# One weight's low part moved from VectorE to GpSimd, and new instruction orders on ScalarE and VectorE

## What is computed

```
def even_mixer(h, w_in, w_out, ...):
    q, k, v, g_att, u_ssm, g_ssm = split(h @ w_in)        # w_in: 1024 x 5120
    q = apply_partial_rope(q) * HEAD_DIM ** -0.5           # the "rotary"
    k = apply_partial_rope(k)
    att = dilated_attention(q, k, v)
    ssm = s5_ssm(u_ssm, a_re, a_im, log_dt, b, c, d_skip, glu_w, glu_b)
    return concat([att * silu(g_att), ssm * silu(g_ssm)]) @ w_out
x = x + rmsnorm(even_mixer(rmsnorm(x)))      # layer 0 of block one
x = x + rmsnorm(odd_mixer(rmsnorm(x)))       # layer 1 of block one
for layer in range(2):                       # block two
    h = h + hybrid_mixer(rms_norm(h), ...)
    h = h + expert_choice_ffn(rms_norm(h), ...)
return rms_norm(h, final_norm_g)
```

## Time and profile before

| | |
|---|---|
| median of 3 runs | 1636.35 us (1635.52 to 1637.13) |
| the profiled execution | 1636.07 us, its span 1634.2 us |
| PE busy | 1307.5 us (80%) |
| DVE / ACT / POOL busy | 574.0 / 453.5 / 137.4 us (35% / 28% / 8%) |
| HBM read | 513.33 MB, 315 GB/s over the span |
| chain that ended last, by engine | DMA 45%, PE 38%, DVE 11%, ACT 2%, issue 2% |

### The profile page before, as it was taken

The page is one execution under the profiler, slowest core; times in us unless marked ns, Lnnn a source line. Parts: engine busy times, 40 slices in busy tenths (PEclk is TensorE's granted clock), DMA queues, the critical chain, the costliest instruction groups (busy, mean ns, idle before and its releaser), DMA issues.

```text
span 1634.2 us, 28359 instructions
## 1 busy us (share of the span) xinstructions
PE 1307.5 (80%) x12516; PEld 923.0 (56%) x12516; DVE 574.0 (35%) x873; ACT 453.5 (28%) x580; POOL 137.4 (8%) x169
## 2 busy tenths in 40 slices
PE   8999999999999987566666667999987556565665
PEld 6789889998989743223222234889843223232232
DVE  7993774765484520000000001584521001000001
ACT  5337654445554311001010012555311001010011
POOL 0220200000314000000000000304000000000000
PEclk9999999999999999988899897999999988899878
DMA  8334344545435899999999999335899999999997
GB/s 279 104 129 155 117 172 155 200 163 204 155 139 197 371 426 426 428 428 428 428 429 428 429 428 405 139 113 222 344 427 427 427 429 429 428 428 428 429 426 301
DMA packets 79503, 515.59 MB, mean 316 GB/s; under 512 B 6544, under 2 KB 6928, under 8 KB 54592
## 3 DMA queue, kind: packets, MB, share of 16 engines
q1 hardware_dynamic: 76000, 509.21, 76.4%
q0 software_dynamic: 912, 2.83, 0.5%
q10 hardware_dynamic: 2512, 2.36, 0.4%
HBM read 513.33 MB, written 1.05 MB: 315 GB/s over the span
## 4 chain that ended last, share of the span: by engine, by line
DMA 45%; PE 38%; DVE 11%; ACT 2%; issue 2%; SPq 1%; DVEq 0%; ACTq 0%
DMA board<-in_w_down 24%; DMA board<-in_w_gate 21%; PE dense L1750 8%; PE dense L1752 8%; PE dense L1751 8%; PE bank L2321 4%; PE bank L2351 2%; DVE ring_parts L1273 2%; DMA ring<-in_even_w_in 1%; DVE board L1556 1%; ACT ring_parts L883 1%; DVE board L1547 1%; PE dense L1773 1%; PE bank L2144 1%; PE bank L2291 1%
## 5 line engine op out<-in xcount | busy, mean ns | idle before, releaser
L2321 PE MATMUL bank<-ring,board 128*32 128x256 f32 x2688 | 207.4, 459 | 145.7 <-DMA ring<-in_w_up 82.5
L2321 PEld LDWEIGHTS bank<-ring,board 128*32 128x32 f32 x2688 | 90.4, 124 | 257.1 <-DMA ring<-in_w_up 104.2
L1107 ACT ACTIVATE board<-bank 128x256 f32<-128x256 f32 x32 | 12.3, 384 | 731.7 <-PE bank L2321 731.7
L1273 DVE TENSOR_TENSOR ring_parts<-ring,ring_parts 128x4096 fp32r<-128x4096 f32 (+1 forms) x43 | 181.6, 4228 | 88.6 <-ACT ring_parts L883 88.5
L1663 DVE TENSOR_TENSOR board<-board,bank 128x256 f32<-128x256 f32 x32 | 13.5, 421 | 553.3 <-ACT board L1107 553.3
L883 ACT ACTIVATE ring_parts<-ring 128x4096 fp32r<-128x4096 f32 (+1 forms) x47 | 161.5, 3438 | 123.7 <-DMA ring<-in_w_in 31.7
L1750 PE MATMUL dense<-board_parts,ring_parts 128*128 128x256 f32 x624 | 179.4, 288 | 0.5 <-DVE ring_parts L1273 0.5
L1752 PE MATMUL dense<-board_parts,ring_parts 128*128 128x256 f32 x624 | 176.6, 283 | 0.0
L2321 PE MATMUL bank<-board 128*32 128x256 f32 x1408 | 108.8, 461 | 65.4 <-DMA board<-in_w_up 40.7
L1750 PEld LDWEIGHTS dense<-board_parts,ring_parts 128*128 128x128 f32 x624 | 119.7, 192 | 1.9 <-issue 1.6
L1752 PEld LDWEIGHTS dense<-board_parts,ring_parts 128*128 128x128 f32 x624 | 119.6, 192 | 0.0
(11 more groups left out here) (354 smaller groups left out, 2057.3 us busy)
## 6 DMA issues: line engine op xcount, KB each, us to landing
ring<-in_w_gate SPq DMA_DIRECT2D x44, 2048.0 KB, 41.4
ring<-in_w_up SPq DMA_DIRECT2D x40, 2048.0 KB, 41.6
ring<-in_w_down SPq DMA_DIRECT2D x40, 2048.0 KB, 41.0
board<-in_w_up SPq DMA_DIRECT2D x24, 2048.0 KB, 41.0
board<-in_w_gate SPq DMA_DIRECT2D x20, 2048.0 KB, 40.5
board<-in_w_down SPq DMA_DIRECT2D x20, 2048.0 KB, 40.7
ring<-in_w_in SPq DMA_DIRECT2D x18, 2048.0 KB, 7.8
ring<-in_even_w_in SPq DMA_DIRECT2D x9, 2048.0 KB, 8.6
```

Source lines behind the costliest of these rows:

```text
L1273: tt(lo, slot_of(u), hi.bitcast(F32), ALU.subtract).then_inc(lo_done, 1)
L2321: last = mm(o.rearrange("p (m b) -> p m b", b=2), xeT[:, 4 * (j // 2) + k, :], cols.rearrange("p (m r b) -> p r m b", r=2, b=2)[:, q % 2], ...
```

## The change

- **Unit 4's low part**: DVE's `low_part(4)` between `whole_block(7)` and `states(0)` is gone. POOL makes it in one `tensor_tensor`, after `hi_done` has counted unit 4 and ahead of the rotary of q, with a signal of its own, for which PE waits before unit 4. The running count `lo_done` leaves unit 4 out.
- **ACT around units 1 and 2**: the copy `u_steps` moves ahead of `high_part(2)`; the three small transfers that ACT issues (masks and router weights) then come before `high_part(2)` too.
- **DVE around units 1 and 2**: the low part of unit 1 moves behind the products of the next round (`times`), and the low part of unit 2 likewise.
- **First seam**: DVE does `add_rows(1)` before tile 0's low part instead of behind it; unit 15's low quarters 0 and 1 move behind tile 1's gain.
- **Second seam**: of the next unit's low quarters, one instead of two stands between `add_rows(1)` and `normalise(1)`.
- **Experts' ends**: ACT's mean square goes by halves (`rms_halves`, L787), each half waiting for its own `x_ready`.

```diff
-            return sum(4 if v in QUARTERED else 1 for v in SPLIT if v <= u)
+            return sum(4 if v in QUARTERED else 1 for v in SPLIT if v <= u and v != POOL_LOW)
...
             gp.wait_ge(rest_in, 16)
+            gp.wait_ge(hi_done, SPLIT.index(POOL_LOW) + 1)
+            hi, lo = slot_of(POOL_LOW, True)
+            g.tensor_tensor(lo, slot_of(POOL_LOW), hi.bitcast(F32), ALU.subtract).then_inc(pool_lo_done, 1)
             for w, t in enumerate((q_tok, k_tok)):
                 gp.wait_ge(dense_out, 3 + 2 * w)
...
             high_part(1)
-            high_part(2)
             act.dma_start(masks[:].rearrange("p l n -> p (l n)"), a["pair_masks"]).then_inc(masks_in, 16)
             for l in range(2):
                 act.dma_start(wr[:, l], a["w_router_2"][l].rearrange("(k p) e -> p k e", p=P)).then_inc(router_in, 16)
             act.wait_ge(unit_done, 1)
             s.activation(u_steps, DP[0][:].rearrange("p z (c b i) -> p (z c) i b", c=2, i=SL), ACT.Copy).then_inc(dense_out, 1)
+            high_part(2)
...
                 for i in range(NT):
-                    act.wait_ge(x_ready, 6 + 6 * l + 2 * (i + 1))
-                    rms(i, x[:, i, :])
+                    at = 6 + 6 * l + 2 * i
+                    rms_halves(i, x[:, i, :].rearrange("p (b n) -> p b n", b=2), (x_ready, at + 1), (x_ready, at + 2))
...
+                add_rows(0, 1)
+                dve.wait_ge(x_ready, 1)
+                dve.wait_ge(sum_half, 1)
+                normalise(0)
+                gain_rows(0, name)
+                add_rows(1, 1)
+                gain_low(0, x_lo)
+                dve.wait_ge(x_ready, 2)
+                dve.wait_ge(sum_half, 2)
+                normalise(1)
+                gain_rows(1, name)
+                low_part(SECOND[0], 0)
+                gain_low(1, x_lo)
+                for n in range(1, 4):
+                    low_part(SECOND[0], n)
...
                 times(z, sm(3), sm(4))
+                if i in (1, 2):
+                    low_part(3 - i)
                 z = pair(B_AT + 32 * i)
                 own.go(tt(z[:, 0], by_re[:, 0], by_im[:, 1], ALU.subtract))
                 own.link(tt(z[:, 1], by_re[:, 1], by_im[:, 0], ALU.add))
-                if i >= 2:
-                    low_part(4 - i)
...
             for t in range(8):
                 whole_block(t)
-            low_part(4)
             states(0)
...
             for i in range(NT):
                 add_rows(i, 2)
-                for n in range(2):
+                for n in range(1 if i else 2):
                     low_part(FIRST2[0] + i, n)
...
-                gain_out(i, "n1_0", x_lo2)
-            for n in range(2, 4):
+                gain_rows(i, "n1_0")
+                gain_low(i, x_lo2)
+            for n in range(1, 4):
                 low_part(FIRST2[0] + 1, n)
...
             def arrived(u):
-                if u in SPLIT:
+                if u == POOL_LOW:
+                    pe.wait_ge(pool_lo_done, 1)
+                elif u in SPLIT:
                     pe.wait_ge(lo_done, vector_lows(u))
```

More of the change, by code:

```diff
@@ L428, in build @@
         QUARTERED = SECOND + [FIRST2[l] + n for l in range(2) for n in (6, 7)]
+        POOL_LOW = 4
         def vector_lows(u):
-            return sum(4 if v in QUARTERED else 1 for v in SPLIT if v <= u)
+            return sum(4 if v in QUARTERED else 1 for v in SPLIT if v <= u and v != POOL_LOW)
         def free_at(t):
@@ L454, in build @@
         lo_done = sem("lo_done")
+        pool_lo_done = sem("pool_lo_done")
         mix_lo_done = sem("mix_lo_done")
@@ L1139, in normalise, with gain_out @@
                     ts(xs[:, i, half], x[:, i, half], rstd[:, i:i + 1], None, ALU.mult).then_inc(xs_ready, 1)
-            def gain_out(i, name, low=None):
+            def gain_out(i, name):
                 for half in range(2):
@@ L1146, in gain_out, with gain_rows, gain_low @@
                     g = vc(name)[:, 4 * half:4 * half + 4].unsqueeze(2).to_broadcast([P, 4, P])
[L1147 to L1151, removed]
                     tt(xT[:, 4 * half:4 * half + 4, i * P:(i + 1) * P],
                        WB[2 * i + half][:].rearrange("p (c s) -> p c s", c=4), g, ALU.mult).then_inc(xT_ready, 1)
-                for half in range(2 if low is not None else 0):
+            def gain_rows(i, name):
+                for half in range(2):
+                    count["xt"] += 1
+                    dve.wait_ge(xt_ps, count["xt"])
+                    c = slice(4 * half, 4 * half + 4)
+                    tt(xs[:].rearrange("p i (c s) -> p c i s", c=DC)[:, c, i, :],
+                       WB[2 * i + half][:].rearrange("p (c s) -> p c s", c=4),
+                       vc(name)[:, c].unsqueeze(2).to_broadcast([P, 4, P]), ALU.mult).then_inc(gained, 1)
+            def gain_low(i, low):
+                for half in range(2):
                     count["hi"] += 1
@@ L1172, in add_rows, with norm_between @@
                     tt(x[:, i, half], x[:, i, half], xs[:, i, half], ALU.add).then_inc((sum_half, x_ready)[b], 1)
[L1174 to L1188, removed]
+            def norm_between(name):
+                dve.wait_ge(row_in, 16)
+                add_rows(0, 1)
[13 more added lines that the diff above has]
+                    low_part(SECOND[0], n)
             def sm(n):
@@ L1424, in _ @@
             low_part(14)
-            norm_between(1, "pre1")
+            norm_between("pre1")
             def pool(g):
```

## The result

The changed kernel takes 1646.23 us (median of 6 runs, 1644.80 to 1647.49); the kernel before took 1636.28 in the same comparison (6 runs, 1635.52 to 1640.55). The ratio is 1.0057, 95% interval 1.0047 to 1.0067: it is slower, by 9.95 us between the medians. Its profiled execution took 1646.12 us, span 1644.0, 9.8 more than the span before.

A forecast was written before the change was run, and what follows sets the result against it. Experts' stages were taken as bound by their bytes, starting when PE's dense stage frees the ring. Terms +7.1 +1.2 +0 -0.5 +0.1 = +7.9 on the profiled 1636.07 gave 1644.0 us, range 1640 to 1647.6.

The forecast's parts named there:

- U's wait: Start of unit 1: putting `u_steps` first removes PE's 2.28 us idle before U, a lead of about 2.0 us.
- DVE's lead: End of unit 2's low part: DVE is 1.9 us ahead (0.5 to 2.3), taking unit 2's slip as 0.5.
- POOL's duration: Unit 4's low part: POOL's subtraction of 4096 columns takes 9.0 us.
- The stop: DVE stands still for POOL's whole 9.0 us before `whole_block`; PE's second triangle starts 7.1 us later (+4.7 to +9.1).
- Rival A: Unit 4's low part: DVE keeps the port or both overlap, so no hold; total -2.7, 1633.4 us; chance 0.14.
- Rival B: POOL gives up the port part way or takes 5 us; DVE loses 3 to 5, 1638 to 1640; chance 0.07.
- Rival C: Unit 2 lands so late that its low part or `bpow_ready` holds PE too: 1648 to 1650; chance 0.04.
- The clock: After PE's 10 us idle the granted clock falls once, slowing the second and third triangles: +1.2 us (0 to 1.7).
- First seam: DVE's swapped pieces: PE loses 0.4 on tile 0's low part, tile 1's earlier gain cancels it: 0 (-0.1 to +0.4).
- Second seam: One low quarter less before `normalise(1)` lets DVE take tile 1's mean sooner: gain 0.5 us (0 to 0.6).
- Ends: Experts' ends, mean square by halves: 0.1 won in layer one, 0.2 lost at kernel's end; +0.1 (-0.1 to +0.3).

The follow-up runs named there:

- e5: Kernel before with only ACT's and DVE's new order around units 1 and 2: 1634.48 us, ratio 0.9989.
- e1: Kernel before with only unit 4's low part moved to POOL, ahead of the rotary: 1648.54 us, ratio 1.0074.
- e4: Changed kernel with unit 4's low part shared, half of the columns on POOL and half on DVE: 1641.11 us, ratio 1.0024.
- e7: Changed kernel with POOL's subtraction cut into four instructions of 1024 columns: 1645.29 us, ratio 1.0053.
- e9: Changed kernel with POOL's subtraction for unit 4 waiting until DVE has written the first eight blocks: 1641.01 us, ratio 1.0030.
- e2: Changed kernel with unit 4's low part back on DVE behind the eight blocks, all other orders kept: 1635.26 us, ratio 0.9986.
- e8: Changed kernel with POOL's subtraction replaced by filling the same place with zeros: 1642.62 us in its one run.

## Why the prediction was right, and what was off

The forecast was 1644.0, by the port's stop; it came out at 1646.2. Step by step:

- **U's wait:** predicted 2.0, measured 2.05 at U. DVE's lead: predicted 1.9, measured 1.65, since unit 2 landed 0.78 later instead of 0.5. e5, with this part alone, is 1.45 early at the router and 1.9 faster by the medians.
- **POOL's duration:** predicted 9.0 (7 to 9.6), measured 8.96. **The stop:** predicted at the next boundary of DVE and for the whole duration; measured 8.79, and in e1, e4, e7 and e9 again. T2 came at 83.20 (predicted 83.1), PE's idle time was 10.18 (predicted almost 10). The Trainium skill's page "SBUF — State Buffer", section "SBUF: two separate sides", calls the port pair that the two engines share an exclusive lock for the whole instruction; the trace agrees at 4096 columns too, 8.79 of 8.96 us.
- **Rival A** (DVE keeps the port, or the two overlap) would have been right without the stop: e2 stands at -2.59 at the router where it had -2.8 (-2.3 - 0.5); at the end, where it had -2.7, 1.3 are left by the medians. Its price was right and its mechanism didn't occur. **Rival B** (a short hold) fell with 8.79. **Rival C** (the front slips further) didn't occur: unit 2 landed 0.78 late, and PE waited nowhere for its low part.
- **The clock:** predicted 1.2 (0 to 1.7), measured 1.73. This step is the term that was mis-sized: "many short products, less tied to the clock" doesn't hold. The part of T2 and T3 at the low level took 3.64 instead of 1.94, 1.88 times, where the experts' products took 1.76 times. What one fall costs also differs from run to run by how long the low level lasts behind the idle time: from T2 on PE lost 1.2 in e1, 1.3 in e8, 1.9 in e7 and 2.5 in e4.
- **First seam:** predicted 0 (-0.1 to +0.4), measured -0.15 over the seam in after (+8.92 before it, +8.77 behind it); L1810, which answers to L1791, came 0.34 late (0.4 predicted). **Second seam:** predicted -0.5, measured -0.65. **Ends:** predicted +0.1, measured +0.17 at the kernel's end. In layer one nothing of this size can be separated.
- **The sum up to the router:** 7.1 + 1.2 + 0 - 0.5 = +7.8, measured +7.92. That it is so close is in part luck: the clock's extra 0.5 went with the second seam's extra gain and 0.35 that came back between 227 and 390 us.
- **What the sum lacks** is what comes after the router, and with it 2 of the 9.95 us: from +7.92 to +9.8 in the profiled executions. I took one trace of before as the measure. Its span of 1634.2 is 0.65 under the mean of 76 other executions of the same kernel (1634.85, from 1632.2 to 1639.5, standard deviation 1.4). Taking for each kernel the mean span of its runs less 1634.85, less its own figure in the table's router column, leaves +1.3 for after, and for the ten others with several runs -0.2 (e5) to +2.4 (e1), mean +1.1, the faster kernels among them. So most of that rest belongs to the trace taken as the measure and to each trace's own scatter, and not to the change. That layer one adds something of its own to a late kernel isn't excluded: that part stays open.

## What to carry to other kernels

Before a piece of VectorE's work goes to GpSimd, compare the two durations on the same operands: 4.43 against 8.96 us here. VectorE stands still for the second figure if what it does next has its operands in SBUF. Here VectorE's own share had been hidden behind TensorE's work, and so the whole stop was lost (8.6 us at T2 in e1). Cutting the piece up (e7) or placing it where nothing waits for VectorE (e9) moved the loss and didn't remove it: in e9 TensorE waited for GpSimd itself, and paid again through the clock. Not tried is a place where VectorE's instructions read PSUM while GpSimd runs. And when a change has several parts, time them apart: here the start's orders gained 1.9 us by the medians, the seams' 0.6, which can't be told from none, and GpSimd's part lost 12.

## What the runs showed that I had not expected

- A tensor-scalar instruction of VectorE with one operand stands still too, and beside a GpSimd instruction that only writes: 3.28 us instead of 0.69 beside a filling of 3.52 (e8). One that reads PSUM doesn't (0.68 beside the subtraction in e9).
- The small instructions of the rotary cost as well: 1.5 us of VectorE over eight instructions, and GpSimd's own take 0.78 to 1.44 (after, e2) where 0.45 is their shortest.
- An idle time of 3.0 us of TensorE cost 2.9 more by the clock behind it (e9).
- Where the clock falls in the router's stretch is worth 1.7 us (10.46 or 12.15 us for the same work). It may be one cause of the scatter of 1.4 us between executions, which is as large as what the good parts of the change give; each kernel has one trace, so this is not shown.
